# Routing of two expert layers: group and best expert in one chain, and GpSimd on the chosen group's maxima and one-hots

## What is computed

```python
def hier_moe(x, rg_w, rg_b, re_w, re_b, w_gu, w_down):
    t = x.reshape(n_tok, D)
    g_prob = jax.nn.softmax((t @ rg_w + rg_b).astype(jnp.float32), axis=-1)          # 4 groups
    g_p, g_idx = lax.top_k(g_prob, 1)
    e_logits = (t @ re_w + re_b).astype(jnp.float32).reshape(n_tok, MOE_GROUPS, MOE_EPG)   # 8 experts a group
    e_logits = jnp.take_along_axis(e_logits, g_idx[:, :, None], axis=1)[:, 0]
    e_p, e_idx = lax.top_k(jax.nn.softmax(e_logits, axis=-1), MOE_TOPK)              # two experts
    e_p = e_p / jnp.sum(e_p, -1, keepdims=True)
    gate = (g_p * e_p).reshape(-1)
    ...
```

## Time and profile before

| | us |
|---|---|
| median of 3 runs | 1944.93 (1942.79 to 1947.19) |
| the profiled execution | 1943.57 |
| its span | 1941.70 |
| TensorE products busy | 1629.4 (84%) |
| VectorE busy | 678.3 (35%) |
| ScalarE busy | 370.5 (19%) |
| GpSimd busy | 194.9 (10%) |
| mean rate of all transfers | 277 GB/s over the span |

### The profile page before, as it was taken

One profiled execution on the slowest core, in us unless ns is written; L12 is line 12 of the kernel. 1 busy time (PEld: TensorE's weight loads), 2 busy tenths in 40 slices (PEclk: granted clock), 3 DMA queues, 4 the chain that ended last, 5 costly groups with the idle time before them and its releaser, 6 DMA issues.

```text
span 1941.7 us, 30728 instructions
## 1 busy us (share of the span) xinstructions
PE 1629.4 (84%) x13306; PEld 1036.1 (53%) x13306; DVE 678.3 (35%) x1148; ACT 370.5 (19%) x746; POOL 194.9 (10%) x91
## 2 busy tenths in 40 slices
PE   9999999999999999866666888999888768675664
PEld 8998986997994865222222333767864223221211
DVE  1565431464532265211111123672465211111103
ACT  1444101343211251000000001332211000000001
POOL 2331422332330000000000000000300000000000
PEclk9999999999999999988988899999999998988887
DMA  9351443252454438999999999322157999999995
GB/s 387 101 173 51 188 182 157 95 151 89 152 195 195 162 131 352 429 426 429 427 427 428 423 426 393 111 87 68 69 210 305 427 427 424 427 427 428 427 427 229
DMA packets 48213, 537.01 MB, mean 277 GB/s; under 512 B 4532, under 2 KB 12980, under 8 KB 15032
## 3 DMA queue, kind: packets, MB, share of 16 engines
q1 hardware_dynamic: 46752, 528.27, 66.5%
q10 hardware_dynamic: 1304, 6.51, 0.9%
HBM read 533.71 MB, written 1.05 MB: 275 GB/s over the span
## 4 chain that ended last, share of the span: by engine, by line
PE 60%; DMA 30%; DVE 6%; ACT 3%; issue 1%; POOL 0%; DVEq 0%; ACTq 0%; POOLq 0%
PE ps L448 48%; DMA arena<-in_moe_w_gu 17%; PE ps L460 9%; DMA ring<-in_moe_w_gu 6%; PE ps L466 2%; DMA ring<-in_moe_w_down 2%; DMA arena<-in_moe_w_down 2%; DMA extra<-in_moe_w_gu 2%; DVE x L1553 1%; DVE arena L1542 1%; ACT arena L2469 1%; ACT arena L2473 1%; DVE hb L1542 1%; DVE arena L1547 1%; DVE arena L1553 0%
## 5 line engine op out<-in xcount | busy, mean ns | idle before, releaser
L460 PE MATMUL ps<-arena 128*32 128x512 f32 (+1 forms) x1348 | 200.3, 676 | 84.3 <-DMA arena<-in_moe_w_gu 64.4
L448 PE MATMUL ps<-hT,ring 128*128 128x256 f32 (+2 forms) x1600 | 266.2, 326 | 0.0
L2473 ACT ACTIVATE arena<-ps 128x512 f32<-128x512 f32 (+4 forms) x152 | 92.3, 607 | 872.0 <-PE ps L460 478.3
L448 PEld LDWEIGHTS ps<-hT,ring 128*128 128x128 f32 (+1 forms) x1600 | 237.0, 187 | 25.5 <-issue 2.1
L460 PE MATMUL ps<-ring,arena 128*32 128x512 f32 x1248 | 170.5, 675 | 87.7 <-DMA ring<-in_moe_w_gu 68.5
L1542 DVE TENSOR_TENSOR arena<-arena,ps 128x256 f32<-128x256 f32 (+3 forms) x110 | 55.6, 506 | 473.8 <-ACT arena L2469 419.6
L448 PE MATMUL ps<-arena 64*64 64x64 f32 (+11 forms) x2000 | 149.1, 299 | 30.2 <-ACT arena L2762 22.3
L460 PEld LDWEIGHTS ps<-arena 128*32 128x32 f32 (+1 forms) x1348 | 48.3, 123 | 216.0 <-issue 94.8
L460 PEld LDWEIGHTS ps<-ring,arena 128*32 128x32 f32 x1248 | 37.2, 117 | 197.8 <-DMA ring<-in_moe_w_gu 97.6
L448 PEld LDWEIGHTS ps<-arena 64*64 64x64 f32 (+4 forms) x2000 | 92.7, 150 | 85.0 <-ACT arena L2762 49.4
L448 PE MATMUL ps<-arena,ring 128*128 128x256 f32 (+2 forms) x928 | 129.8, 319 | 2.9 <-ACT hT L2473 1.4
(11 more groups left out here) (205 smaller groups left out, 1826.0 us busy)
## 6 DMA issues: line engine op xcount, KB each, us to landing
arena<-in_moe_w_gu SPq DMA_DIRECT2D x57, 2048.0 KB, 41.3
ring<-in_moe_w_gu SPq DMA_DIRECT2D x49, 2048.0 KB, 40.4
ring<-in_moe_w_down SPq DMA_DIRECT2D x35, 2048.0 KB, 40.6
arena<-in_moe_w_down SPq DMA_DIRECT2D x29, 2048.0 KB, 40.6
extra<-in_moe_w_gu SPq DMA_DIRECT2D x22, 2048.0 KB, 40.8
ring<-in_w_merge SPq DMA_DIRECT2D x16, 2048.0 KB, 8.0
ring<-in_w_in SPq DMA_DIRECT2D x9, 2048.0 KB, 7.4
ring<-in_attn_w_qkv SPq DMA_DIRECT2D x6, 2048.0 KB, 7.4
```

What stands on the lines that cost most here:

```text
L448: i = t.matmul(o, l, r, start=first, stop=last, skip_group_check=True)
L460: i = t.matmul(o, l, r, start=first, stop=last, skip_group_check=True)
L2473: s.activation(o, a, ACT.Copy).then_inc(*act.one(name))
```

## The change

The router columns are laid out with the 32 expert logits first and the 4 group logits behind them, and four values of -1e30 fill them up to 40: five groups of 8. One maximum over the five groups gives each group's best expert and the best group; one `first_of` gives the first position of each; a fused instruction pushes these down, and a second maximum and `first_of` give each group's second best. VectorE adds the one-hots for all four groups and multiplies with the chosen group's one-hot, so `sel` is as before. The instructions that found the group alone and masked the other groups' logits go.

The best and the second logit of the chosen group, which the gates need, are now made by GpSimd from the maxima of all groups: for each a product with the chosen group's one-hot and two additions of halves, then the difference, seven instructions. ScalarE waits for the last of them (`margin`) between its two exponentials. Behind `sel` GpSimd also multiplies the two one-hot tables with the chosen group's (two instructions over 2 x 32 values), and `gates_of` on VectorE waits for them (`kept`). `gate_in` keeps one of its two subtractions. The table `rog` goes.

```diff
@@ memory @@
+    e.lo, e.eq, e.k1, e.k2, e.e2 = (carve(80).rearrange("p (t n) -> p t n", t=NT) for _ in range(5))
+    e.ex = carve(64).rearrange("p (t n) -> p t n", t=NT)
+    e.top, e.next, e.ix = (carve(10).rearrange("p (t g) -> p t g", t=NT) for _ in range(3))
+    e.own, e.two = carve(8).rearrange("p (t g) -> p t g", t=NT), carve(4).rearrange("p (t g) -> p t g", t=NT)
+    e.gp, e.m1, e.m2 = (carve(2) for _ in range(3))
@@ vector_program, route @@
+        lo5, k15, k25, e25, eq5 = (a.rearrange("p t (g n) -> p t g n", g=5) for a in (e.lo, e.k1, e.k2, e.e2, e.eq))
+        sel4, rising = e.sel.rearrange("p t (g n) -> p t g n", g=4), tab["roe"][:, 0:8].unsqueeze(1).unsqueeze(1)
+        def first_of(dst, val, top):
+            tt(eq5, val, each(top), ALU.is_ge)
+            tt(eq5, eq5, bc(rising, [P, NT, 5, 8]), MUL)
+            red(e.ix, eq5, MAX)
+            tt(dst, eq5, each(e.ix), ALU.is_equal)
+        ms(e.lo[:, :, 36:40], NEG)
         for i in tiles:
             v.wait_ge(*pe(M + f"route{i}"))
-            tt(e.lo[:, i], ps(M + f"route{i}")[:, 0:36], rrow("mb", 36, 36 * l), ADD, M + f"logits{i}")
-        red(e.mx, gl, MAX)
-        first_of(e.g_oh, gl, e.eq[:, :, 0:4], tab["rog"], 4, e.mx, ALU.is_lt)
-        stt(e.em.rearrange("p t (g n) -> p t g n", g=4), bc(e.g_oh.unsqueeze(3), [P, NT, 4, 8]), NEG, el, MUL, ADD)
-        red(e.m1, e.em, MAX)
-        first_of(e.k1, e.em, e.eq, tab["roe"], 32, e.m1, ALU.is_equal)
-        stt(e.e2, e.k1, 2 * NEG, e.em, MUL, ADD)
-        red(e.m2, e.e2, MAX)
-        first_of(e.k2, e.e2, e.eq, tab["roe"], 32, e.m2, ALU.is_equal)
-        tt(e.sel, e.k1, e.k2, ADD, M + "sel")
+            tt(e.lo[:, i, 0:36], ps(M + f"route{i}")[:, 0:36], rrow("mb", 36, 36 * l), ADD, M + f"logits{i}")
+        red(e.top, lo5, MAX)
+        first_of(k15, lo5, e.top)
+        stt(e25, k15, 2 * NEG, lo5, MUL, ADD)
+        red(e.next, e25, MAX, M + "tops")
+        first_of(k25, e25, e.next)
+        tt(e.sel, e.k1[:, :, 0:32], e.k2[:, :, 0:32], ADD)
+        tt(sel4, sel4, bc(e.k1[:, :, 32:36].unsqueeze(3), [P, NT, 4, 8]), MUL, M + "sel")
@@ vector_program, gate_in and gates_of @@
-        tt(e.ex[:, :, 0:4], e.lo[:, :, 0:4], bc(e.mx.unsqueeze(2), [P, 2, 4]), SUB)
-        tt(e.m2, e.m2, e.m1, SUB, M + "gates in")
+        tt(e.ex[:, :, 0:4], e.lo[:, :, 32:36], bc(e.top[:, :, 4:5], [P, 2, 4]), SUB, M + "gates in")
...
+        v.wait_ge(*pool(M + "kept"))
         tt(o1, o1, col(e.m1, 32), MUL)
@@ scalar_program, moe @@
         fn(g4, g4, ACT.Exp)
+        s.wait_ge(*m.pool(M + "margin"))
         fn(e.m2, e.m2, ACT.Exp, M + "gates exp")
@@ gpsimd_program @@
+    def chosen(l):
+
+        e, M = m.moe, f"moe{l} "
+        keep = e.k1[:, :, 32:36]
+        g.wait_ge(*dve(M + "tops"))
+        for o, a in ((e.m1, e.top), (e.m2, e.next)):
+            both(e.own, a[:, :, 0:4], keep, MUL)
+            both(e.two, e.own[:, :, 0:2], e.own[:, :, 2:4], ADD)
+            both(o, e.two[:, :, 0], e.two[:, :, 1], ADD)
+        both(e.m2, e.m2, e.m1, SUB, M + "margin")
+        g.wait_ge(*dve(M + "sel"))
+        for k, name in ((e.k1, None), (e.k2, M + "kept")):
+            k4 = k[:, :, 0:32].rearrange("p t (g n) -> p t g n", g=4)
+            both(k4, k4, bc(keep.unsqueeze(3), [P, NT, 4, 8]), MUL, name)
...
         g.memset(m.moe.acc, 0.0).then_inc(*pool.one(M + "acc zero"))
+        chosen(l)
```

More of the change, by code:

```diff
@@ L84, in tables @@
     out["i64"] = (a == b).astype(float)
-    out["rog"] = np.tile(1000.0 - np.arange(4.0), (P, 1))
     out["ios"] = np.tile(np.arange(96.0), (P, 1))
@@ L2013, in route, with each @@
+        sel4, rising = e.sel.rearrange("p t (g n) -> p t g n", g=4), tab["roe"][:, 0:8].unsqueeze(1).unsqueeze(1)
+        def each(a):
+            return bc(a.unsqueeze(3), [P, NT, 5, 8])
+        def first_of(dst, val, top):
[4 more added lines that the diff above has]
+        ms(e.lo[:, :, 36:40], NEG)
         for i in tiles:
             v.wait_ge(*pe(M + f"route{i}"))
-            tt(e.lo[:, i], ps(M + f"route{i}")[:, 0:36], rrow("mb", 36, 36 * l), ADD, M + f"logits{i}")
@@ L2032, in gates_of @@
     def gates_of(l):
         e, M = m.moe, f"moe{l} "
-        o1, o2 = e.k1, e.k2
+        o1, o2 = e.k1[:, :, 0:32], e.k2[:, :, 0:32]
         def col(a, n):
@@ L3316, in layout @@
         "lam": i["attn_lambda_2"].reshape(-1),
-        "mb": np.concatenate([i["moe_rg_b_2"], i["moe_re_b_2"]], axis=1).reshape(-1), "nb2v": i["nsa_b2"][:, 1].reshape(-1),
+        "mb": np.concatenate([i["moe_re_b_2"], i["moe_rg_b_2"]], axis=1).reshape(-1), "nb2v": i["nsa_b2"][:, 1].reshape(-1),
     }
@@ L3328, in layout @@
         "cz0": tabs["cz0"], "cz1": tabs["cz1"],
-        "wr": np.concatenate([i["moe_rg_w_2"], i["moe_re_w_2"]], axis=2).reshape(2, KT, P, 36).transpose(2, 0, 1, 3).reshape(P, -1),
+        "wr": np.concatenate([i["moe_re_w_2"], i["moe_rg_w_2"]], axis=2).reshape(2, KT, P, 36).transpose(2, 0, 1, 3).reshape(P, -1),
         "lora1": packed(np.concatenate([i["rw_w1_2"][0], i["rw_a1_2"][0], i["rw_g1_2"][0]], axis=1), (288,)),
```

## The result

| | before | after |
|---|---|---|
| median of 8 runs each | 1943.68 us | 1954.89 us |
| lowest to highest | 1940.4 to 1947.19 | 1950.15 to 1957.22 |
| ratio, 95% interval | | 1.0057 [1.0043, 1.0071] |
| profiled execution, its span | 1943.57, 1941.7 | 1956.81, 1955.0 |

The changed kernel is slower by 0.57%, about 11 us. The forecast was 1943.9 us with a range up to 1947.5. So the range did not hold the time, and the side was wrong too.

The account below looks back on a forecast made before the run. The expert stages' weight streams were taken as the bound, their start waiting on VectorE's exposed choice. Saving 0.81 less 0.3 contention, 0.51 us a layer, 1.0 in all, gave 1944.93 - 1.0 = 1943.9 us, range 1941.3 to 1947.5.

Parts of the forecast that it names:

- What bounds the kernel: Expert stages: weight streams start only after routing, so every us by which TensorE's first round starts earlier starts the stream earlier.
- The choice on VectorE: Group and expert choice between second logits and count: 4.36 us shortened to 3.55, saving 0.81 us a layer.
- GpSimd's price: GpSimd's instructions in the choice: estimated 0.19 us for a small one, 0.31 over 64 elements.
- The slack: ScalarE's second exponential and copy after GpSimd's seven steps: 1.8 us to spare before that wait ends last.
- the moment of need: When ScalarE's second exponential must have GpSimd's result so the copy is not delayed: 759.1.
- giving way to VectorE: GpSimd's seven steps beside VectorE's choice: some 0.9 us added to their 1.9, so done at 757.3.
- The rival of the dear small instruction: GpSimd's small instructions in the choice: at 1.27 us each, 4.7 us lost a layer, 1954.3 us; chance 0.08.
- Contention: Shared port in the choice's second half and first one-hots: GpSimd delays VectorE by 0.2 + 0.1 = 0.3 us a layer.
- The blocking row: Profile evidence for the shared port: a VectorE product beside a GpSimd instruction took 1.86 us, otherwise 0.19.
- full alternation: Rival, shared port: each of five VectorE instructions loses a whole GpSimd step, the one-hots too; 1946.6 us, chance 0.15.
- the sum: Both layers' routing: 0.81 - 0.3 = 0.51 us saved a layer, twice is 1.0 us.
- The clock's rival: TensorE's granted clock, 0.92 in 1140 to 1160 us, in our favour: 1.6 us for that stretch; 1940 us, chance 0.07.

Follow-up runs that it names:

- e7: Changed kernel with never-executed instructions for placement, plus 20 small VectorE memsets in series ahead of the first maximum in each layer; 1949.19 us, 1.0026 of the kernel before.
- the well-placed kernels: Changed kernel with never-executed VectorE instructions that put its rare bodies in a good place, seven comparisons; ratios 0.9982 to 0.9997 of the kernel before, mean 0.9990.
- e1: Changed kernel with eight never-executed VectorE instructions, so the rare bodies lie where they lie in the kernel before; 1944.05 us, 0.9997 of the kernel before.
- e2: Kernel before with 120 never-executed VectorE instructions, so later bodies lie by the same remainder of 128 as in the changed kernel; 1958.04 us, 1.0067.
- e3: Changed kernel with two never-executed VectorE instructions ahead of the later pairs' rare bodies; 1954.76 us, 1.0043 of the kernel before.
- e5: Changed kernel with forty never-executed VectorE instructions ahead of the later pairs' rare bodies; 1941.4 us, 0.9985 of the kernel before.
- e4: Changed kernel with three never-executed VectorE instructions ahead of the later pairs' rare bodies; 1941.1 us, 0.9982 of the kernel before.
- e11: The kernel of e4 measured once more: changed kernel with three never-executed VectorE instructions; 1943.11 us, 0.9992 of the kernel before.

## Why the prediction was wrong

**What bounds the kernel: right.** The first issue of the weight stream is 1.34 us earlier, of which 0.48 was there ahead of the routing (second logits at 751.82 instead of 752.30) and 0.86 is the change's; e7 shows that a delay of the routing is carried to the end. That a gain is carried too rests on the well-placed kernels, some 2 us faster where 1.6 were saved, at the edge of what the runs can tell.

**The choice on VectorE: right to the hundredth.** 0.81 us saved was worked out, 0.81 measured. A step over 80 elements is 0.27 to 0.28 us (752.05 to 752.32, 752.32 to 752.60), worked out 0.275.

**GpSimd's price: right.** Its groups by shape (count | busy us, mean ns):

```profile
L3020 POOL TENSOR_TENSOR arena<-arena 128x64 f32<-128x64 f32 x4 | 1.2, 297 | 0.4
L3020 POOL TENSOR_TENSOR arena<-arena 128x2 f32<-128x2 f32 x6 | 1.2, 194 | 0.5
```

The straight line through the 512- and 1024-element forms gave 0.31 and 0.19. The slack that was put at 1.8 us is 2.6. The second maxima (754.0 instead of 754.46) and the moment of need (758.6 instead of 759.1) are both 0.5 earlier, with the second logits; what is new is the 0.9 us for giving way to VectorE, which did not come: the seven instructions took 1.9 us, 754.02 to 755.94. The rival of the dear small instruction has no ground left.

**Contention: too high by all of it.** 0.3 us a layer was put in. The last five instructions of the choice, four of them with two operands in SBUF, ran beside GpSimd and none was stretched (three in 0.76 us, so 0.26 from start to start). The blocking row was for a GpSimd instruction of 2.3 us; with instructions of 0.2 us nothing of it can be seen. So full alternation, which the Trainium skill, "SBUF — State Buffer", section "Who interferes with whom", would give if taken at its word, did not happen. Without this term the sum is 2 x 0.81 = 1.6 us, 1943.3 us, which the runs can't tell from the 1943.9 forecast.

**The failed step.** The prediction costed one shift, that of later buffers by 16 bytes, "at nothing, since no row here shows a price of position", and of the other shift it said nothing: the removed instructions shorten VectorE's program, and all code behind them moves. The sum went over what is executed and left out where it lies. Its price is the 12.48 instead of 1.38 us at pair 14, 8.05 us of idle TensorE and some 5 us of work at the lower clock behind it, about 13 us in the profiled pair of executions; e1 gives it back and e2 makes it in a kernel without the change. In the medians it is 11 us. With the code in a good place the sum holds: e1 has 1944.05 us, closer to 1943.9 than such runs can tell (its interval is 0.28% wide), and the seven well-placed runs lie between 1941.1 and 1944.1.

There was a row that could have told. The kernel before has 18.3 us of "issue" ahead of three VectorE instructions, with 10.4 the longest, shown above; it was not looked for, because the prediction read only waits on its own chain. The Trainium skill, "Runtime: NRT & Kernel Launch", section "Instruction fetch mechanics", states the rule: a taken branch whose target is not in the window of fetched pages makes the engine wait for a DMA. This case's traces agree with it (5.3 to 6.8 us behind far jumps), and differ in the block: the packets of that queue are 8192 bytes here, and the page has 16 KiB.

**The clock's rival** stood in the forecast as a gain by chance. It came in as a loss, and as a follower: the granted clock fell to 0.86 behind the 8.05 us of idle time that the stall made.

## What to carry to other kernels

An edit that adds or removes instructions moves all code behind it. Where a kernel jumps to far bodies while its DMA queues are full, look for "issue" ahead of the first instruction behind each jump, and ask for each whether another engine waits there. Before an edit is blamed or praised for half a per cent, put the same number of never-executed instructions back, ahead of those bodies, and measure again; and if a stall of that kind is on the path, a few such instructions are the cheapest mend, though a fragile one, since the next edit moves the bodies again and other input data take other bodies.

## What the runs showed of the hardware

A jump into code that is not at hand cost VectorE 5.3 to 6.8 us while the weight stream held the DMA engines at a share of 0.98 to 1.02; a second fetch behind it 3.8 to 4.9. At the kernel's end, with the share at 0.35, VectorE's last jump cost 2.7 to 3.1. The jump to pair 14 was free (1.4 to 1.9 us up to the one-hots, with the flags' reads in it) in all kernels but after, e2 and e3; in e5, by the count of blocks, its code had been fetched ahead by the rare body entered some 75 us earlier and never executed. The way back from pair 12's body to the main program stalled too, 5.3 to 5.8 us, in the kernel before, after and e1 to e4, and from pair 14's 5.8 to 5.9 in after, e2 and e3. The latter cost nothing: VectorE's wait for ScalarE there is 7.57 us with it (after) and without it (before). The step between the two is one instruction: 1954.76 us in e3, 1941.1 in e4 and 1943.11 in its repetition e11.

A stall of 5 to 10 us on VectorE costs nothing that can be measured where TensorE waits for weights (pairs 12 and, in layer 1, 5), and where it does not, it costs more than itself: 8.05 us of idle time on TensorE were followed by 32 products in 7.09 instead of 3.79 us.

GpSimd's products over 2 to 8 elements take 0.19 to 0.23 us with 0.28 us start to start, close to VectorE's own small instructions of 0.16 to 0.17 us with 0.20.
